# Layer 0's first RMS scales computed per token and spread by diagonal matmuls, in a two-layer S5 and pooling trunk

## What is computed

```python
def rmsnorm(x, g):
    return x * lax.rsqrt(jnp.mean(x * x, axis=-1, keepdims=True) + 1e-5) * g

def trunk_layer(x, ...):
    proj = rmsnorm(x, g_mix) @ w_in            # 1024 -> 1024
    y_a = s5_mixer(proj[..., :512], ...)       # complex diagonal scan, GELU, half-GLU
    y_b = pool_mixer(proj[..., 512:], ...)     # trailing-window means minus the token, small matmuls
    x = x + concat([y_a, y_b]) @ w_out
    x = x + square(relu(rmsnorm(x, g_ffn) @ w_ff1)) @ w_ff2
# two layers, then a final rmsnorm; the states and pooling histories are outputs too
```

## Time and profile before

| | us |
|---|---|
| three executions | 2159.89, 2159.79, 2155.44 |
| their median | 2159.79 |
| the profiled execution, its own time | 2159.76 |
| its span in the trace | 2157.9 |
| its time outside the span | 1.9 |

### The profile page before, as it was taken

The page is one execution under the profiler, slowest core; times in us unless marked ns, Lnnn a source line. Parts: engine busy times, 40 slices in busy tenths (PEclk is TensorE's granted clock), DMA queues, the critical chain, the costliest instruction groups (busy, mean ns, idle before and its releaser), DMA issues.

```text
span 2157.9 us, 29004 instructions
## 1 busy us (share of the span) xinstructions
PE 2085.5 (97%) x12894; PEld 2044.8 (95%) x12894; DVE 1092.7 (51%) x1459; ACT 439.2 (20%) x525; POOL 145.0 (7%) x171
## 2 busy tenths in 40 slices
PE   6989899999999999999999999999999999999997
PEld 6878899999999999999989899999999999999997
DVE  7889555364644435353466745643333434343346
ACT  5222342020111111011232233311010101111112
POOL 0022020000000000000020300200000000000003
PEclk9999999999999999999999999999999999999998
DMA  4526311111111121113124461111111111111112
GB/s 151 153 85 171 93 49 45 49 44 46 69 62 59 49 62 59 51 59 121 68 103 129 120 186 39 40 49 40 49 40 49 43 46 44 45 46 43 48 41 83
DMA packets 68861, 152.64 MB, mean 71 GB/s; under 512 B 8288, under 2 KB 28544, under 8 KB 68352
## 3 DMA queue, kind: packets, MB, share of 16 engines
q1 hardware_dynamic: 49264, 112.63, 16.6%
q0 software_dynamic: 7664, 24.65, 3.8%
q10 hardware_dynamic: 11808, 13.51, 2.1%
HBM read 123.23 MB, written 27.53 MB: 70 GB/s over the span
## 4 chain that ended last, share of the span: by engine, by line
PE 82%; DVE 10%; ACT 4%; issue 2%; DMA 1%; ACTq 0%; SPq 0%; DVEq 0%
PE tile L448 77%; PE tile L714 2%; DVE h_low L1037 2%; DVE x L1384 2%; DVE w_low L1033 1%; ACT h_high L763 1%; ACT w_high L748 1%; DVE dve_products_late L1023 1%; DVE pool_s L1023 1%; PE small L616 1%; PE small L610 1%; DMA w_raw<-w_blocks 1%; PE small L501 1%; DVE states L1023 0%; DVE prep_products L1023 0%
## 5 line engine op out<-in xcount | busy, mean ns | idle before, releaser
L448 PE MATMUL tile<-h_high,w_high 128*128 128x408 f32 (+1 forms) x1920 | 427.5, 331 | 22.3 <-DVE h_low L1037 19.6
L1384 DVE TENSOR_TENSOR x<-tile,x 128x816 f32<-128x816 f32 (+1 forms) x304 | 205.7, 718 | 456.1 <-PE tile L448 440.2
L448 PE MATMUL tile<-h_low,w_high 128*128 128x408 f32 (+1 forms) x1920 | 423.1, 328 | 0.0
L448 PE MATMUL tile<-h_high,w_low 128*128 128x408 f32 (+1 forms) x1920 | 422.8, 328 | 0.0
L448 PEld LDWEIGHTS tile<-h_high,w_high 128*128 128x128 f32 x1920 | 320.9, 188 | 28.6 <-issue 19.0
L748 ACT ACTIVATE w_high<-w_raw 128x1024 fp32r<-128x1024 f32 x162 | 170.4, 1052 | 746.6 <-PE tile L448 728.6
L448 PEld LDWEIGHTS tile<-h_low,w_high 128*128 128x128 f32 x1920 | 320.6, 188 | 1.1
L448 PEld LDWEIGHTS tile<-h_high,w_low 128*128 128x128 f32 x1920 | 320.4, 188 | 1.0
L448 PE MATMUL tile<-hidden_high,w_high 128*128 128x408 f32 (+1 forms) x1440 | 318.3, 329 | 2.1 <-DVE x L1384 1.2
L448 PE MATMUL tile<-hidden_low,w_high 128*128 128x408 f32 (+1 forms) x1440 | 316.3, 328 | 0.0
L448 PE MATMUL tile<-hidden_high,w_low 128*128 128x408 f32 (+1 forms) x1440 | 316.3, 328 | 0.0
(11 more groups left out here) (195 smaller groups left out, 1670.5 us busy)
## 6 DMA issues: line engine op xcount, KB each, us to landing
w_raw<-w_blocks SPq DMA_DIRECT2D x164, 512.0 KB, 3.5
x<-x_t ACTq DMA_DIRECT2D x8, 544.0 KB, 11.6
u_blocks<-ua_dram SPq DMA_DIRECT2D x64, 68.0 KB, 2.7
ya_dram<-u_blocks ACTq DMA_DIRECT2D x64, 68.0 KB, 2.7
y_a<-ya_dram POOLq DMA_DIRECT2D x8, 544.0 KB, 4.4
x_kept<-x ACTq DMA_DIRECT2D x8, 544.0 KB, 2.7
cy_dram<-y_quarter POOLq DMA_DIRECT2D x16, 256.0 KB, 2.9
carry_weights<-cy_dram POOLq DMA_DIRECT2D x8, 512.0 KB, 6.8
```

What stands on the lines that cost most here:

```text
L448: mm = pe.matmul(ps[tile][:, c, 0:(b - a) * J], lhs, xt[:, k, a * J:b * J], start=(first and n == 0), stop=(last and n == 2))
L1384: ins = v.tensor_tensor(xt, pt_, xt, ALU.add)
```

## The change

The other norms keep the old way. For layer 0's first norm:

- PE (`token_sums`) multiplies with `rms` as the stationary operand, 128 tokens at a time, and one column of ones: nine matmuls (TB = 9, the last with 64 tokens) of one column each, into column i of a PSUM tile. So the sum of a token lies in one partition, and there are nine values to a partition. They stand where `sum_part` 0 and 1 stood.
- ACT (`token_roots`) takes the square root of 128 x 8 and of 64 x 1; DVE (`token_inverse`, put inside `discretised(0)`) the reciprocal of 128 x 9.
- ACT (`diagonal`, behind `split_hi(2)`) makes nine 128 x 128 diagonal matrices: the identity times the token's scale.
- PE (`spread`, three matmuls behind tile 1, with `diag_made` 9 ahead of them) multiplies all-ones with the diagonals, in chunks of 408, 408 and 272 columns: the scales in all partitions.
- ACT (`spread_out`, between `raw_tile(1)` and `split_hi(3)`) copies them to `rms`. DVE waits for the last copy, then goes on with `first_u(0)`.

`small_numbers()` has four entries at its start where it had three.

```diff
@@ small_numbers
-    sums(0)
+    order.append("token sums")
+    order.extend(("spread", c) for c in range(3))
@@ buffers, in the place of later data
+        by_token = at("rstd_by_token", G + 4352 + TB * P, [P, TB])
+        diag = at("rstd_diagonal", G + 4352, [P, TB * P])
@@ PE
+            def token_sums():
+                out = small_at(SM["token sums"])
+                pe.wait_ge(first_added, KD - 1)
+                for i in range(TB):
+                    n = min(P, T - P * i)
+                    mm = pe.matmul(out[0:n, i:i + 1], rms[:, P * i:P * i + n], ones[:, 0:1], start=True, stop=True)
+                mm.then_inc(small_done, 1)
+            def spread(c):
+                a, b = CHUNKS[c]
+                out = small_at(SM["spread", c])
+                pe.wait_ge(diag_made, TB)
+                pe.matmul(out[:, 0:(b - a) * J], ones[:, :], diag[:, a * J:b * J],
+                          start=True, stop=True).then_inc(small_done, 1)
@@ first_tiles
                         if k == KD - 1:
-                            sum_part(0, 0)
-                            sum_part(0, 1)
+                            token_sums()
                         mm = products(0, 0, k, k, hhi, hlo, k == 0, k == KD - 1)
                         if k == KD - 1:
                             mm.then_inc(tile_done, 1)
-                            sum_part(0, 2)
...
                     products(1, 1, KD - 1, KD - 1, hhi, hlo, False, True).then_inc(tile_done, 1)
+                    for c in range(3):
+                        spread(c)
@@ ACT
+            def token_roots():
+                n = SM["token sums"]
+                act.wait_ge(small_done, n + 1)
+                for rows, cols in ((slice(0, P), slice(0, TB - 1)), (slice(0, T % P), slice(TB - 1, TB))):
+                    ins = act.activation(by_token[rows, cols], sm[n % 2][rows, cols], ACT.Sqrt,
+                                         scale=1.0 / DM, bias=eps_col[rows, :])
+                ins.then_inc(small_free, 1)
+            def diagonal():
+                act.wait_ge(rstd, 3)
+                act.wait_ge(bc_in, 16)
+                for i in range(TB):
+                    act.activation(diag[:, P * i:P * i + P], prep_of[0].pp[:, C_ID:C_ID + P], ACT.Copy,
+                                   scale=by_token[:, i:i + 1]).then_inc(diag_made, 1)
+            def spread_out():
+                for c, (a, b) in enumerate(CHUNKS):
+                    n = SM["spread", c]
+                    act.wait_ge(small_done, n + 1)
+                    act.activation(rms[:, a * J:b * J], sm[n % 2][:, 0:(b - a) * J], ACT.Copy).then_inc(small_free, 1)
@@ ACT, layer loop
                     if l == 0 and t == 0:
-                        roots(0)
+                        token_roots()
                     if l == 0 and t < 2:
                         raw_tile(t)
+                    if l == 0 and t == 1:
+                        spread_out()
                     ahead(LB + t + 2, LT + t)
+                    if l == 0 and t == 0:
+                        diagonal()
@@ DVE
+            def token_inverse():
+                v.wait_ge(small_free, SM["token sums"] + 1 + 2)
+                v.reciprocal(by_token[:, :], by_token[:, :]).then_inc(rstd, 3)
@@ discretised, ahead of the products that make bbar_re and bbar_im
+                if l == 0:
+                    token_inverse()
@@ DVE, start and layer 0
+            v.memset(by_token[:, :], 1.0).then_inc(ones_set, 1)
                     split_lo(2)
-                    inverse(0)
+                    v.wait_ge(small_free, SM["spread", 2] + 1 + 2)
                     first_u(0)
```

More of the change, by code:

```diff
@@ L21 @@
 T = BLK * J
+TB = -(-T // 128)
 KD = DM // P
@@ L251, in hybrid_trunk @@
         rstd = sem("rstd")
+        diag_made = sem("diag_made")
         ones_set = sem("ones_set")
@@ L522, in drives @@
                     mm.then_inc(small_done, 1)
-            pe.wait_ge(ones_set, 1)
+            pe.wait_ge(ones_set, 2)
             for l in range(LAYERS):
@@ L848, in _ @@
                 act.activation(((tr, ts)[m % 2] if m else rms)[:, :], x[:, m, :], ACT.Square).then_inc(sq_made, 1)
-            act.wait_ge(ones_set, 1)
+            act.wait_ge(ones_set, 2)
             def raw_tile(t):
```

## The result

| | us |
|---|---|
| the change, median of 15 executions | 2162.39 (2159.62 to 2164.59) |
| the kernel before, 15 executions beside it | 2158.38 (2155.44 to 2160.69) |
| ratio, 95% interval | 1.0017 [1.0009, 1.0025] |
| the profiled execution of the change: own time, span | 2164.59, 2162.8 |

The forecast was 2159.1 with a range up to 2161.9. The change is slower by 0.17%, and its 2162.39 is outside. The forecast stood on a before of 2159.76; the 15 executions beside the change have their median 1.4 us lower, so against them the forecast move is -0.6 and the measured one +4.0.

What follows compares the result with a forecast made beforehand. PE was taken to bound the kernel (busy 97%). Tile 2 starting 3.2 us later, against a 3.8 us prize of removed idleness and low clock, gave -0.6 us from 2159.76: 2159.1, range 2155.8 to 2161.9.

Steps and rivals of the forecast that it cites:

- Token sums: PE from 38.43 us: 18 one-column passes at 0.11 us take 2.0 us, bounds 1.1 and 3.4.
- table load and roots: ACT after the token sums: 1.28 us table load ends at 41.9, two tiny square roots end at 42.35 us.
- nine diagonals: ACT: nine 128-column activations of 0.29 us each, 2.65 us taken, ending at 47.0; bounds 1.0 and 3.5 us.
- tile 2 starts: PE, after waiting for diagonals and three spreads: starts at 49.3 us, 3.2 us later than 46.11.
- x_quart no longer waited for: DVE result ahead of PE's first transposes: comes at about 57.5 us, so PE's 2.28 us of idleness go.
- no low clock behind the transposes: PE, transposes and tile 3 after tile 2: full clock, 13.1 us; the low clock had taken 1.5 us.
- the prize: PE around the first transposes: 2.28 us of idleness plus 1.5 us of low clock, 3.8 us at most.
- tile 1: PE, two k steps of 2.97 us after the token sums and tile 0: ends at 45.0 us.
- Rival A: PE's wait for the diagonals, 45 to 47 us: clock falls there, costing 1.5 us; +0.9, 2160.7; chance 0.28.
- Rival B: ACT's diagonals cheap, 1.0 us for nine: tile 2 starts at 47.7, in all -2.2, 2157.6; chance 0.15.
- Everything behind follows PE: 0.6 us earlier: All work behind tile 3: moves up with PE, tile 3 ending at 74.6 us against 75.18.
- Rival C: Later low-clock stretches: a shift may add or save falls of 1.5 us each, up to 4 us either way; chance 0.12.

Runs made afterwards that it cites:

- no_recip: Kernel before without layer 0's large reciprocals, tokens scaled with the root instead of its inverse: median 2155.60 us, ratio 0.9983.
- The kernels cut at 150 us: Kernel before and changed kernel, each ended behind layer 0's last input tile: medians 156.36 us before, 156.27 us with the change.
- its two padded kernels: Kernel before with 18 or 36 unused two-column matmuls at the start of PE's program: medians 2161.17 and 2161.15 us, ratios 1.0005 and 1.0010.
- the same 37 as above: Executions of the change, the change repeated unedited, and the change with 18 unused matmuls at PE's start: mean 2162.4 ± 0.2 us.
- the kernels cut at 310 us: Both kernels ended behind layer 0's mixer: medians 336.37 us before, 340.12 changed; before with 18 unused matmuls 340.74, change with 110 339.81.
- weights_first: Kernel before with `drive_weights(0, 0)` and `split_lo(3)` moved ahead of the reciprocals on DVE: median 2161.36 us, ratio 1.0009.
- dummy_tokens: Kernel before with nine unused token sums (18 one-column passes) behind the last column sum, scales made the old way: median 2162.42 us, ratio 1.0013.

## Why the prediction was wrong

**Right, by its own steps.** Token sums 2.12 for 2.0; table load and roots done at 42.2 for 42.35; nine diagonals 2.73 for 2.65, so neither end of the bounds; tile 2 starts at 49.18 for 49.3; x_quart no longer waited for; no low clock behind the transposes. no_recip confirms the prize at 3.7 us. The change was to be 0.6 us ahead behind tile 3, and the two profiles have 0.9 and 0.5. The kernels cut at 150 us neither confirm nor exclude that. Missed, but hidden: tile 1 ended 1.6 us late.

**Rival A** half came: the clock did fall, but behind the token sums and not in the wait for the diagonals, and that wait covered its cost. **Rival B** didn't come.

**The step that failed** is "Everything behind follows PE: 0.6 us earlier". From 300 to 1000 us the work did only shift, as the prediction says ("that stretch can only shift"); but between 150 and 310 us, and in the profiles near 1228 us and at the end, it didn't follow. Behind 112 us a shift changes the work's place against two things that don't shift with it.

1. The instruction packets. They follow the number of instructions, not the time. I counted the 18 passes as 2.0 us of PE and did not count them as 36 instructions in front of all that follows. Shifted packets alone cost 1.9 ± 0.3 us in the full kernel. One meeting is seen, at 229.6 us, and delays PE by 0.8 us in the traces, 1.7 with the low clock behind it. No run moved this packet and no other, so that the whole 1.9 comes by it is not shown.
2. The clock. PE waits at about 151, 161, 215, 250 and 1227 us in both kernels, and whether the clock falls behind such a wait, and for how long, differs from execution to execution. From the mean granted clock of every execution, the time at the lower level is 32.0 ± 0.3 us before (130 executions), 33.6 ± 0.6 in its two padded kernels, and 37.3 ± 0.7 in the change (the same 37 as above; 35.4, 37.7 and 39.3 in its three sets). At the lower level nearly half of the work is lost where PE has work (in the change three matmuls of a k step take 0.91 us at 43 us and 0.50 at 50 us), so the change's 5.3 us more are at most an estimated 2.6 us, and the padded kernels' 1.6 us an estimated 0.8. This is a correlation over executions. Which part of the edit does it, and why more falls come with it on average, no run has shown.

The two overlap, since the 1.9 holds the padded kernels' own low clock. Without counting that twice: -0.7 for the edit's gain in its profiles, +1.9 for the shifted packets, and half of 37.3 - 33.6, +1.8, for the clock that is left, give +3.0, and the pooled means are 3.2 apart. That this closes is no proof of the last term, and the kernels cut at 310 us contradict a clean sum. What is shown: in the cut kernels the loss comes between 150 and 310 us; shifting PE's instruction packets brings about half of the full kernel's loss; and 110 unused matmuls in the idle start take 1.7 ± 0.6 us of it away. The cause of the other half stays open.

**Rival C** named the kind of cause ("something later answers") and had 0.12, centred on no change. That centring was the second error: the kernel before happens to have its packets clear of that landing, and each of the seven full kernels that added 36 or more PE instructions without putting the packets back came out slower than it by median. That isn't the only way to lose: weights_first adds none, has the short landing in its trace, and is slower by median too. Rows for such a suspicion were at hand: the landing that POOL waits for and the instruction queue stand in the trace of before.

No version beat both kernels, apart from no_recip, which leaves work out.

## What to carry to other kernels

When an edit adds or removes many instructions on an engine with a long straight program, its instruction packets move against all later work. Look up the instruction queue in the trace, and the short transfers that something waits for, and ask which will meet; here that place was nearly 200 us behind the edit. And before believing a fraction of a per cent, pad the old kernel with as many unused instructions in an idle place: here that alone was worth more than the change was meant to gain.

## What the runs showed of the hardware

- A one-column f32 matmul with a stationary 128x128 costs two passes of 0.118 us (18 in 2.12 us), hardly more than the 0.11 us of a transpose pass, which moves 128 columns. That the weight loads set the pace of both is likely and not shown. By the Trainium skill ("TensorE: Matmul & The Clock Gate", LDWEIGHTS), column count over 1.2 GHz, such a load is an estimated 107 ns, and the trace is a tenth above that.
- Behind those 18 passes (38.31 to 40.43) the clock was 0.50 from 41.6 to 45.0 in the profile of the change, with no wait of PE longer than 0.88 us since its first product at 13.60. It fell between 39.7 and 41.6 us in five of the eight traces that have them in a row in this place. In dummy_tokens, with 18 such passes a little later, it stayed 1.00.
- Behind the same 1.97 us of idleness near 1228 us the clock stays 1.00 in five of the 14 full kernels' traces and falls to 0.50 in nine (the window at 1229.50 above is one). The same wait is no fixed price.
- A 16 KB instruction packet near this store takes 0.9 to 1.8 us (up to 2.3 elsewhere). Where it starts 0.8 to 1.2 us behind the issue, the 32 KB store lands 1.5 to 1.9 us later, as POOL sees it: the last two of its 32 packets start when the instruction packet ends.
